# Extra multiplications of constants on TensorE while it stands in the norms

## The reference

```python
def modulated_sublayer(x, mod, g_pre, g_post, fn, weight):
    shift, scale, gate = mod[:, 0], mod[:, 1], mod[:, 2]
    h = rmsnorm(x, g_pre) * (1.0 + scale) + shift
    y = rmsnorm(fn(h), g_post)
    return x + weight * (1.0 + gate) * y

# layer 0: swiglu, pool_mixer, swiglu;  layer 1: swiglu, mla_mixer, swiglu
# then:    x + mixer(rms_norm(x)),  x + moe(rms_norm(x))
```

## Time and profile before

| | |
|---|---|
| median of 3 runs | 2018.83 us (2018.33 to 2025.63) |
| profiled execution: time, span | 2018.54 us, 2016.7 us |
| TensorE busy | 1838.0 us, 91% of the span, 13471 records |
| VectorE, ScalarE, GpSimd busy | 988.3 us (49%), 665.3 us (33%), 21.6 us (1%) |
| mean granted clock of TensorE | 0.945 |
| bytes moved | 483.15 MB, 240 GB/s |

### The profile page before, as it was taken

The page is one execution under the profiler, slowest core; times in us unless marked ns, Lnnn a source line. Parts: engine busy times, 40 slices in busy tenths (PEclk is TensorE's granted clock), DMA queues, the critical chain, the costliest instruction groups (busy, mean ns, idle before and its releaser), DMA issues.

```text
span 2016.7 us, 32388 instructions
## 1 busy us (share of the span) xinstructions
PE 1838.0 (91%) x13471; PEld 1516.9 (75%) x13471; DVE 988.3 (49%) x1398; ACT 665.3 (33%) x962; POOL 21.6 (1%) x14
## 2 busy tenths in 40 slices
PE   6999949999799988989998899988886999999998
PEld 3999938999799976779997799877873444434443
DVE  2977569886674545264455776456523111111111
ACT  3433324443434434354444533445411000000000
POOL 0000000000000000000000111000000000000000
PEclk8999968999899989989997999989987999999999
DMA  9988507887384421245441332422333999999996
GB/s 389 391 332 322 221 32 275 337 334 277 120 345 180 175 104 63 104 179 188 178 175 55 124 108 108 194 95 94 130 122 142 422 425 425 426 427 426 426 426 284
DMA packets 44589, 483.15 MB, mean 240 GB/s; under 512 B 4944, under 2 KB 5200, under 8 KB 5200
## 3 DMA queue, kind: packets, MB, share of 16 engines
q1 hardware_dynamic: 44352, 480.74, 60.4%
q10 hardware_dynamic: 144, 1.05, 0.1%
HBM read 480.72 MB, written 1.05 MB: 239 GB/s over the span
## 4 chain that ended last, share of the span: by engine, by line
PE 40%; DMA 8%; DVE 5%; ACT 2%; issue 1%; DVEq 0%; SPq 0%; ACTq 0%
PE psG L370 23%; PE psA L370 10%; DMA ring<-stream 8%; PE psS L370 5%; DVE parts L2099 1%; ACT parts L1482 0%; DVE mem L2114 0%; ACT mem L1649 0%; PE psS L1148 0%; DVE sg L2135 0%; PE psS L1022 0%; DVE mem L1948 0%; DVE mem L1942 0%; DVE mem L2381 0%; PE psG L1198 0%
## 5 line engine op out<-in xcount | busy, mean ns | idle before, releaser
L370 PE MATMUL psG<-parts 128*128 128x256 f32 x6016 | 787.2, 291 | 26.9 <-issue 9.0
L370 PEld LDWEIGHTS psG<-parts 128*128 128x128 f32 x6016 | 762.9, 199 | 37.9 <-issue 22.2
L370 PE MATMUL psA<-parts 128*128 128x256 f32 x2112 | 267.1, 283 | 0.0
L370 PEld LDWEIGHTS psA<-parts 128*128 128x128 f32 x2112 | 259.5, 192 | 0.0
L1774 DVE TENSOR_TENSOR parts<-ring,parts 128x2048 fp32r<-128x2048 f32 x84 | 192.2, 2288 | 115.1 <-ACT parts L1326 114.6
L370 PE MATMUL psS<-ring,mem 128*64 128x512 f32 (+1 forms) x1032 | 229.5, 594 | 12.7 <-DMA ring<-stream 11.0
L1326 ACT ACTIVATE parts<-ring 128x2048 fp32r<-128x2048 f32 x84 | 160.9, 1915 | 110.9 <-PE psA L370 110.9
L370 PEld LDWEIGHTS psS<-ring,mem 128*64 128x64 f32 (+1 forms) x1032 | 72.8, 137 | 164.9 <-issue 131.9
L1765 DVE SCALAR_TENSOR_TENSOR mem<-ring,silc,mem 128x1536 f32<-128x1536 f32 (+1 forms) x98 | 138.9, 1417 | 2.5
L2099 DVE TENSOR_TENSOR parts<-ring,parts 128x1024 fp32r<-128x1024 f32 x76 | 95.2, 1257 | 86.3 <-ACT parts L1482 85.2
L1697 ACT ACTIVATE mem<-psS 128x512 f32<-128x512 f32 x16 | 9.6, 597 | 367.9 <-PE psS L370 367.9
(11 more groups left out here) (335 smaller groups left out, 1418.8 us busy)
## 6 DMA issues: line engine op xcount, KB each, us to landing
ring<-stream SPq DMA_DIRECT2D x304, 1536.0 KB, 8.9
X<-x_in SPq DMA_DIRECT2D x1, 1024.0 KB, 17.5
mem<-masks ACTq DMA_DIRECT2D x1, 1024.0 KB, 4.7
x_out<-X SPq DMA_DIRECT2D x1, 1024.0 KB, 3.9
cst<-consts SPq DMA_DIRECT2D x1, 240.0 KB, 2.8
cols<-cols_in SPq DMA_DIRECT2D x1, 224.0 KB, 2.6
```

What stands on the lines that cost most here:

```text
L370: return nc.tensor.matmul(out, lhsT, rhs, start=start, stop=stop, skip_group_check=True)
```

## The change

A helper `idle(n)` issues n fp32 multiplications of `ones` (128 by 128) by the first 256 columns of the constants into the first half of `psG`'s second bank; nobody reads what they leave, and no semaphore moves. They are placed ahead of waits: 3 ahead of the wait of every `spread`, 8 ahead of the first `squares` of every pre-norm but the first, 2 ahead of each of its other three waits, 2 at the head of every post-norm, and 4 ahead of the first wait of every FFN.

```diff
+            def idle(n):
+
+                for _ in range(n):
+                    mm(psG[:, 1, 0:S], ones, cst[:, 0:S], start=True, stop=True)
+
...
             def spread(n, post):
 
+                idle(3)
                 pe.wait_ge(sem("norm_inv"), norm_at(n, post) + 1)
...
             def pre_sums(n):
+                if n:
+                    idle(8)
                 for k in range(KT):
                     if k % 2 == 0:
+                        if n and k:
+                            idle(2)
                         pe.wait_ge(sem("pre_sq"), 4 * n + k // 2 + 1)
...
             def post_norm(n):
+                idle(2)
                 for i, k in enumerate((0, 1, 2, 3, 4, 5, 6, 7) if n == 1 else (0, 1, 2, 3, 6, 7, 4, 5)):
...
+                    idle(4)
                     pe.wait_ge(sem("hi_gu"), t0 + 1)
                     if t0 >= 2:
                         pe.wait_ge(sem("act_ready"), t0 - 1)
```

## The result

The changed kernel takes 2028.66 us (median of 5 runs, 2026.06 to 2030.21) where the kernel before takes 2020.06 (5 runs): ratio 1.0042, 95% interval 1.0028 to 1.0057. It is 8.6 us slower, not the 3.6 that was forecast. The profiled execution has a span of 2026.2 us, 9.5 more than before.

A forecast was written before the change was run, and what follows sets the result against it. TensorE (91% busy) mostly sets the end, but norms are one chain across three engines, whose delays pass on one to one. Terms sum to +3.6 us on 2018.5: 2022.1 us, 8 in 10 within 2011 to 2034.

The forecast's parts named there:

- One constant multiplication, 0.427 us: Each fp32 constant multiplication, two records, takes 0.427 us at full clock and 0.85 us at half clock.
- Pre-norm 1 to 6: Constants delay the second spread by 1.06 us, full clock returns 0.87; net +0.2 us each, +1.2 together, bounds 0.3 to 3.6.
- Pre-norm 7: Last pre-norm: constants have no room between its sums; spread starts 2.7 us later, less 0.87 us: +1.8 us.
- Where it has no cover: Kernel's start: the first spread has no wait, so its three constants are pure delay, +1.3 us.
- Post-norms: Number 0 -0.45 us, number 3 -0.8, number 1 behind the pool +0.3, those behind sublayers 2, 4 and 5 +0.3 together.
- the even chance of a lost clock: Post-norm behind the pool: +1.5 us if the clock is lost again among the sums, -0.8 if not; taken as +0.3.
- FFN starts: VectorE's chain covers the four constants; longer pauses may cost two second gate_ups the clock: +1.2 us together, bounds 0 and 2.4.
- MLA, hybrid, router: Gains from a held clock: MLA -0.75 us (1.5 or 0), hybrid -0.3 (bounds 0 and 2.2), router -0.2.
- Rival A: Clock is lost once in each section all the same: 3 us for each of six, +18 us, 2040 us; chance 0.15.
- Rival B: Constants hide in the waits and the clock is full throughout: -17.7 us, 2001 us; chance 0.07.

## Why the prediction was right in kind and short in size

The forecast was 2022.1 us and no change beyond 0.5%; it came to 2028.66, in the range, on the slow side of the band. The direction and the reason were right. That the time lies within the band is partly luck: the largest term left its own bounds, and the band held it because it also had room for gains and losses that did not come. By its own steps:

- **One constant multiplication, 0.427 us.** Right: the cycles grow by 0.43 for each, 16 records take 3.67 us, up to twice that where the clock is lost (2.93 us for three).
- **Pre-norm 1 to 6, +0.2 us each, sum +1.2, bounds 0.3 to 3.6.** This step failed, and outside its bounds: +1.0 to +1.1 in five of them, +0.4 in the one behind the pool, +5.8 together. The mechanism was right (the constants outlast the waits, the spread gives 0.9 back). The mis-sized number is the change-over, taken as 0.05 us a pair, a cycle of 1.17 us. Measured, a cycle is 1.42 us, of which the change-over there and back is about 0.30, 0.25 more than allowed, four times a pre-norm: +1.0. Its upper bound of 0.15 was no bound. I took the nearest seamless rows for it, but the trace of the kernel before had the price, in the MLA at full clock, where weights of 64 columns stand ahead of weights of 128 with no wait between:

```profile
793.07 1.08 PE L370 MATMUL psS<-mem 128*64 128x256 f32 x8
794.08 1.99 PE L370 MATMUL psS<-mem,ring 128*128 128x256 f32 x8
```

There the first wide record starts 0.31 us behind the last narrow one and the second 0.32 behind that, where the streams are 0.216 apart: 0.2 us lost on this side alone (starts of single records, program output).
- **Pre-norm 7, +1.8.** Same cause: +2.9. Its spread started 3.9 us later against the first X, not 2.7.
- **Where it has no cover, +1.3.** The first spread begins 1.4 us after its three constants do, with no wait; the stretch shows +0.8, within what the start varies. No time here settles the term.
- **Post-norms.** -0.45, -0.8 and +0.1 each: measured -0.5, -0.7 and +0.1. Behind the pool the even chance of a lost clock fell badly, +1.0; the half clock is seen in the second window. Nothing that was varied decides it: of the nine kernels with constants but none between the pool's sums, the clock held there in four (2.09 to 2.30 us from root to row) and fell in five (3.87 to 3.97).
- **FFN starts.** The first gate_up doesn't matter, right. The pause ahead of the second grew to 2.34 us in all, and one of two lost its clock: +1.5 in the fourth FFN, 0 in the second, for +1.2. Two terms were not in the sum: in the first FFN the clock was half for longer than before, +1.2, and the third FFN had one stretch of half clock less, -1.4. They cancel by luck.
- **MLA, hybrid, router.** The MLA: -0.75 forecast, -0.9 measured. The hybrid: -0.4 for -0.3, its slots' 72 records still at half clock (10.67 us against the earlier trace rows). The router and the experts: -0.3 for -0.2.
- **Rival A** happened in the change in one section of six, behind the pool; it was brought about by leaving out the head's constants, and then cost 0.6 to 1.5 us a pre-norm, less than the 3 us a section that I gave it. **Rival B** failed by the order of TensorE's queue: the clock was held and the gain was there, 0.7 us between root and row, but the constants ahead of the real work cost more. The Trainium skill's rule in TensorE: Matmul & The Clock Gate (Step-by-step: what each phase is for), multiplications in program order, is what the dose of one, two and three constants shows (0.99, 1.42, 1.85 us a cycle). The Trainium skill's rule on pauses in TensorE: Matmul & The Clock Gate (Why this matters for your kernels) also holds here in direction: with more of the pauses filled the kernel takes 2009 us. But short pauses alone were no safety: with five constants at the head the clock fell at 527 us, though no wait of that pre-norm was longer than 0.77 us.

Open: when the clock falls inside a layer. Each fall costs an FFN 1.3 to 1.5 us or, where the half clock lasted twice as long, up to 2.6, which is why the kernels with one and with three constants between the pairs missed their expected totals though their norms' rows met them; what decides their number and place in an execution, no run here shows.

## What to carry to other kernels

Filling a wait of TensorE to keep its clock costs nothing only if the filler, with its change-over, ends before the awaited work is ready; since multiplications run in program order, every excess is a delay of the chain. A filler that is too short loses the clock, and what follows then takes up to twice as long (2.93 us instead of 1.56 for three). Count the change-over per repetition: four times 0.25 us too little a norm was nearly the whole miss of the pre-norms. Look in the trace for the nearest change of weight width, not for the nearest seamless run. Put filler in the long waits at the edges (the head of a norm, ahead of a second gate_up), not between short steps, and none where the data are already there.

## What the hardware showed unexpectedly

- A change between weights of 128 and of 32 columns cost about 0.30 us there and back: with one, two and three constants of 0.43 us the cycle is 0.99, 1.42 and 1.85 us, and with the filler 32 columns wide too it fell from 1.42 to 1.09 us.
- The norms' own short work did not hold the clock: in the kernel without the head's constants it was full at 526 to 529, where TensorE had 0.35 us of work, and half from 531, behind the sums. With two between the pairs, constants with a quarter of the output columns held it.
- Nor did products of 32 streamed columns at the hybrid's start, though TensorE hardly stood: in the changed kernel they began at full clock at 1092.27 and took 5.79 us behind a wait of 0.67, and the clock fell under them at 1096:

```profile
1095.00:1103.00 8.00, 7.32 (x38) 0.57 0.01 2
```
- In an FFN each stretch of half clock cost 1.3 to 1.5 us (2.6 where it was twice as long), and filling one pause could move the fall rather than remove it (first FFN: 216.0 and 216.1 us).
